# Attention in pairs of maps, with the second layer's conditioning computed inside the feed-forward stages

## The reference, cut to what matters

```
h = rms_norm(x) @ w_in          # latent c_q, c_kv, k_rope; diff q, k, v; gqa q, k, v
diff: 4 heads, each 2 maps, dim 64, value width 128
      a = softmax(q0 k0 / 8) - lam * softmax(q1 k1 / 8);  o = head_rms_norm(a @ v)
gqa:  6 query heads, 2 key/value heads, dim 64;           o = softmax(q k / 8) @ v
mla:  6 heads, q and k of dim 96, value width 64;         o = softmax(q k / sqrt(96)) @ v
x = x + concat(o) @ w_o                                   # 1280 -> 1024
x = x + (silu(xn @ w_gate) * (xn @ w_up)) @ w_down        # hidden 2816
```

## Time and profile before

| | us |
|---|---|
| median of 3 runs | 3374.56 (3374.51 to 3377.14) |
| the profiled execution's own time | 3376.07 |
| its span | 3374.3 |
| PE busy | 3199.8 (95%) |
| DVE, ACT, POOL busy | 1123.0, 994.6, 280.0 |
| chain that ended last | PE 89%, DVE 5%, ACT 4% |

### The profile page before, as it was taken

The page is one execution under the profiler, slowest core; times in us unless marked ns, Lnnn a source line. Parts: engine busy times, 40 slices in busy tenths (PEclk is TensorE's granted clock), DMA queues, the critical chain, the costliest instruction groups (busy, mean ns, idle before and its releaser), DMA issues.

```text
span 3374.3 us, 35084 instructions
## 1 busy us (share of the span) xinstructions
PE 3199.8 (95%) x14020; PEld 2222.0 (66%) x14020; DVE 1123.0 (33%) x1827; ACT 994.6 (29%) x1607; POOL 280.0 (8%) x268
## 2 busy tenths in 40 slices
PE   7999999999989999989999899979999899989997
PEld 6866564788878655648888655544666544468886
DVE  2624331433226243323332223342533300043322
ACT  3345451222233554412222133331322200022222
POOL 4481000000023610000000000000000000000000
PEclk7989999999989999999999899989999899989998
DMA  5221121332322211113323211000111122123331
GB/s 107 77 71 38 51 76 35 90 100 85 95 72 77 83 38 38 60 57 100 100 82 93 77 38 38 25 26 25 40 48 49 27 75 75 50 75 96 88 94 60
DMA packets 340274, 221.98 MB, mean 66 GB/s; under 512 B 8364, under 2 KB 334892, under 8 KB 340112
## 3 DMA queue, kind: packets, MB, share of 16 engines
q1 hardware_dynamic: 337360, 214.65, 22.0%
q0 software_dynamic: 2224, 2.99, 0.8%
q10 hardware_dynamic: 528, 2.10, 0.2%
HBM read 217.62 MB, written 2.10 MB: 65 GB/s over the span
## 4 chain that ended last, share of the span: by engine, by line
PE 89%; DVE 5%; ACT 4%; issue 1%; DMA 1%; DVEq 0%; ACTq 0%; SPq 0%
PE ps L591 83%; PE ps L602 4%; PE ps L618 2%; DVE R L1691 1%; ACT R L1204 1%; DVE xL L1687 0%; DVE x_lows L1687 0%; DMA ident<-in_c_ident 0%; PE ps L945 0%; DMA R<-in_ctx 0%; ACT R L1200 0%; ACT L1193 0%; DVE R L1780 0%; DVE R L1762 0%; DVE wL L1713 0%
## 5 line engine op out<-in xcount | busy, mean ns | idle before, releaser
L591 PE MATMUL ps<-R 128*128 128x64 f32 (+6 forms) x2272 | 519.8, 373 | 29.5 <-ACT R L1204 8.7
L591 PEld LDWEIGHTS ps<-R 128*128 128x128 f32 (+3 forms) x2272 | 306.7, 193 | 244.1 <-issue 138.1
L591 PE MATMUL ps<-xH,wH 128*128 128x512 f32 x1056 | 416.8, 395 | 22.1 <-DVE xL L1687 22.1
L1204 ACT ACTIVATE R<-ps 128x512 f32<-128x512 f32 (+9 forms) x504 | 248.4, 493 | 579.2 <-PE ps L591 514.5
L591 PE MATMUL ps<-U,ring 128*128 128x512 f32 (+5 forms) x960 | 406.3, 575 | 12.3 <-ACT R L1410 12.3
L591 PE MATMUL ps<-xL,wH 128*128 128x512 f32 x1056 | 413.7, 392 | 0.0
L591 PE MATMUL ps<-xH,wL 128*128 128x512 f32 x1056 | 413.6, 392 | 0.0
L1354 ACT ACTIVATE wH<-raws 128x2048 fp32r<-128x2048 f32 (+1 forms) x114 | 192.9, 1692 | 568.3 <-PE ps L591 567.7
L591 PEld LDWEIGHTS ps<-U,ring 128*128 128x128 f32 (+2 forms) x960 | 179.1, 191 | 207.7 <-issue 182.6
L591 PE MATMUL ps<-R,ring 128*128 128x512 f32 x704 | 311.6, 594 | 2.9 <-DVE R L1930 1.6
L1713 DVE TENSOR_TENSOR wL<-raws,wH 128x2048 fp32r<-128x2048 f32 (+1 forms) x114 | 229.3, 2011 | 233.3 <-ACT wH L1354 226.4
(11 more groups left out here) (279 smaller groups left out, 3296.1 us busy)
## 6 DMA issues: line engine op xcount, KB each, us to landing
raws<-in_w_gate_up SPq DMA_DIRECT2D x88, 512.0 KB, 5.1
ring<-in_w_in SPq DMA_DIRECT2D x36, 1024.0 KB, 6.0
ring<-in_w_ada SPq DMA_DIRECT2D x24, 1024.0 KB, 5.2
raws<-in_w_down SPq DMA_DIRECT2D x32, 704.0 KB, 4.6
raws<-in_w_ffn_in SPq DMA_DIRECT2D x44, 512.0 KB, 5.2
ring<-in_w_in SPq DMA_DIRECT2D x34, 512.0 KB, 5.6
raws<-in_w_ffn_out SPq DMA_DIRECT2D x16, 704.0 KB, 4.7
ring<-in_w_o SPq DMA_DIRECT2D x5, 1280.0 KB, 5.8
```

Source lines behind the costliest of these rows:

```text
L591: return nc.tensor.matmul(o, a, b, start=first, stop=last)
L1204: ap.do(f(dst, src, ACT.Copy), sem)
```

## The change

Attention works on pairs of maps: the two maps of a diff head, or two heads of gqa or mla, for 128 queries. That gives 16 + 12 + 12 = 40 pairs p per layer.

- **Scores.** The transposed q and k (`items`) are split like the FFN's operands, high by ACT (L1378), low by DVE, into `QK_parts`. A pair takes six fp32r matmuls of 512 columns instead of two f32 ones. In diff and gqa (dim 64) the two maps lie in the two row halves of the array and alternate. A pair writes both banks of one of two score tiles.
- **Probabilities.** In diff, DVE forms P0 + ratio P1 before the transposes, so that one map is transposed and multiplied. In gqa and mla, POOL multiplies the pair by its inverse sums (`weigh`, L624), and ACT and DVE each copy one transposed map.
- **Values.** In gqa and mla V is the stationary operand. The two heads write the two column halves of a bank, which so holds the transposed output that w_o reads. Only the four diff tiles are still transposed.
- **Order.** For each p PE has scores(p+2), probabilities(p-1), values(p-2), then the transposes of later heads (`BESIDE`) that stood between the stages. ACT has exponentials(p), the copy of p-1, and in diff the output of p-2.
- **w_in.** gqa's pieces come before the latent and diff v ones, diff head 0 is transposed after the first diff v piece, and POOL's gqa rotations stand between its last low parts.
- **Conditioning.** It leaves attention and the ring. In the FFNs of the first block, steps 5 to 36, SP loads 64 pieces of 512 KB into two halves of `spare`. POOL multiplies each by cvec and adds its eight parts to one, PE sums over the rows with one f32 matmul against a column of ones, and ACT copies one column.
- **Banks.** ACT has two PSUM banks in the first block instead of three, and three again in the second.

```diff
+        BESIDE = {-2: ["dq0", "dk0"], -1: ["dq1"], 0: ["dk1"], 3: ["dq2"], 4: ["dk2"], 7: ["dq3"], 8: ["dk3"],
+                  10: ["gk"], 11: ["gq0"], 12: ["gq1"], 13: ["gq2"],
+                  18: ["mq0"], 20: ["mk0"], 22: ["mq1"], 24: ["mk1"],
+                  26: ["mq2", "mk2"], 27: ["mq3"], 28: ["mk3"], 30: ["mq4", "mk4"], 31: ["mq5"], 32: ["mk5"]}
...
-        A_BANKS, D_BANKS, S_BANKS = psum[0:3], psum[3:5], psum[5:8]
+        psum = [ctx.enter_context(nc.psum_tensor(f"ps{i}", [P, 512], F32)) for i in range(4)]
+        SP = [ctx.enter_context(nc.psum_tensor(f"scores{i}", [P, 2, 512], F32)) for i in range(2)]
+        A_BANKS, D_BANKS = psum[0:2], psum[2:4]
...
+        ADA = [(m, 0) for m in range(16)] + [(m, 1) for m in range(16)] + [(m, 0) for m in range(16, 48)]
+        ADA_FIRST, N_ADA = 5, len(ADA) // L
...
-        W_IN = (quarter_pieces("diff_qk", c1, 2 * BH * BV) + quarter_pieces("latent", 0, c1)
-                + quarter_pieces("diff_v", c1 + 2 * BH * BV, BH * BV)
-                + quarter_pieces("gqa_q", c1 + 3 * BH * BV, GH * GD)
-                + quarter_pieces("gqa_kv", c1 + 3 * BH * BV + GH * GD, 2 * GK * GD))
...
+        W_IN = (quarter_pieces("diff_qk", c1, 2 * BH * BV)
+                + [("gqa_q", G0, GH // 2 * GD), ("gqa_q", G0 + GH // 2 * GD, GH // 2 * GD), ("gqa_kv", G0 + GH * GD, 2 * GK * GD)]
+                + quarter_pieces("latent", 0, c1)
+                + quarter_pieces("diff_v", c1 + 2 * BH * BV, BH * BV))
...
+            def weigh(l, p_):
+                a = l * N_PAIR + p_
+                r = 2 * (a % 4)
+                pg.more(sums_inverted)
+                pg.do(nc.gpsimd.tensor_tensor(PX[a % 3], PX[a % 3], bc(rinv[:, r:r + 2], S, 2), ALU.mult), weighted)
...
+            def conditioning(l):
+                pool.wait_ge(cs_ready, 1)
+                for a in range(l * N_ADA, (l + 1) * N_ADA):
+                    w = ada_half(a)
+                    pool.wait_ge(ada_in[a % 2], 16 * (a // 2 + 1))
+                    w_ = w.rearrange("p (k c) -> p k c", k=KT)
+                    pg.do(nc.gpsimd.tensor_tensor(w_, w_, bc(cvec[:, :, ADA[a][1]], P, 2), ALU.mult))
+                    for n_ in (4, 2, 1):
+                        pg.do(nc.gpsimd.tensor_tensor(w[:, 0:n_ * P], w[:, 0:n_ * P], w[:, n_ * P:2 * n_ * P], ALU.add),
+                              ada_summed if n_ == 1 else None)
...
+                    if j >= 9:
+                        rotate(pg, nc.gpsimd, j - 9, Tg, rsG, gtmp, 8, GD, gG, ropeG, gT_ready, l, 6, True)
+                rotate(pg, nc.gpsimd, 3, Tg, rsG, gtmp, 8, GD, gG, ropeG, gT_ready, l, 6, True)
...
+            def modulation(a):
+                pe.wait_ge(ada_summed, a + 1)
+                if a >= 1:
+                    pe.wait_ge(ada_read, a)
+                mm(SP[1][:, 1, 0:1], ada_half(a)[:, 0:P], ones[:, 0:1], True, True).then_inc(ada_full, 1)
...
+                def scores(p_):
+                    a, t = first + p_, p_ % TT
+                    if a >= 2:
+                        pe.wait_ge(s_exp, a - 1)
+                    pe.wait_ge(qk_ready, done + items_needed(p_))
+                    q_k, o, tok = pair_items(p_), SP[a % 2], slice(t * P, (t + 1) * P)
+                    if len(q_k) == 1:
+                        (qh, ql), (kh, kl) = [ITEM_SLOTS[item] for item in q_k[0]]
+                        for n, (q, k) in enumerate(((qh, kh), (qh, kl), (ql, kh))):
+                            for c in range(2):
+                                r = slice(c * BD, (c + 1) * BD)
+                                ins = mm(o[:, c, :], QKP[r, q, tok], QKP[r, k, :], n == 0, n == 2)
+                    else:
+                        for c in range(2):
+                            (qh, ql), (kh, kl) = [ITEM_SLOTS[item] for item in q_k[c]]
+                            for n, (q, k) in enumerate(((qh, kh), (qh, kl), (ql, kh))):
+                                ins = mm(o[:, c, :], QKP[0:AQK, q, tok], QKP[0:AQK, k, :], n == 0, n == 2)
...
+                def probabilities(p_):
+                    a = first + p_
+                    if FAMILY[p_] == "diff":
+                        pe.wait_ge(combined, l * N_DIFF + p_ + 1)
+                    else:
+                        pe.wait_ge(weighted, l * (N_PAIR - N_DIFF) + p_ - N_DIFF + 1)
+                    for c in range(1 if FAMILY[p_] == "diff" else 2):
+                        bank = A_BANKS[c]
+                        pe.wait_ge(*released[id(bank)])
+                        for s_ in range(TT):
+                            ins = nc.tensor.transpose(bank[:, s_ * P:(s_ + 1) * P], PX[a % 3][:, c, s_ * P:(s_ + 1) * P], ident[:, :])
+                        ins.then_inc(pt_full, 1)
+                        released[id(bank)] = (pt_act, a + 1) if c == 0 else (pt_dve, l * (N_PAIR - N_DIFF) + p_ - N_DIFF + 1)
...
+                def values(p_):
+                    a, i, t = first + p_, p_ // TT, p_ % TT
+                    pt = PT[a % 2]
+                    pe.wait_ge(pt_act, a + 1)
+                    if FAMILY[p_] == "diff":
+                        bank = D_BANKS[p_ % 2]
+                        pe.wait_ge(*released[id(bank)])
+                        group(None, bank[:, 0:BV], [(pt[:, 0, s_ * P:(s_ + 1) * P], V[:, s_, VB + i * BV:VB + (i + 1) * BV])
+                                                    for s_ in range(TT)]).then_inc(v_full, 1)
+                        released[id(bank)] = (v_done, v0 + p_ + 1)
+                        return
+                    n = (p_ - N_DIFF) // TT
+                    bank = D_BANKS[0]
+                    pe.wait_ge(pt_dve, l * (N_PAIR - N_DIFF) + p_ - N_DIFF + 1)
+                    if t == 0:
+                        pe.wait_ge(*released[id(bank)])
+                    for s_ in range(TT):
+                        for c in range(2):
+                            at_ = VG + c * GD if FAMILY[p_] == "gqa" else VA + (2 * (i - BH - GH // 2) + c) * AV
+                            ins = mm(bank[c * AV:(c + 1) * AV, t * P:(t + 1) * P], V[:, s_, at_:at_ + AV],
...
+                for p_ in range(N_PAIR + 2):
+                    if p_ + 2 < N_PAIR:
+                        scores(p_ + 2)
+                    if 1 <= p_ <= N_PAIR:
+                        probabilities(p_ - 1)
+                    if p_ >= 2:
+                        values(p_ - 2)
+                    beside(p_)
+                    if p_ in DIFF_OUTPUTS_AT:
+                        diff_outputs(DIFF_OUTPUTS_AT.index(p_))
...
-                pp.more(bT_ready, TT)
-                for h in range(8):
-                    transposes([T[:, t, h * P:(h + 1) * P] for t in range(TT)], P)
+                    if what == "diff_v" and a == V_AT:
+                        pp.more(bT_ready, TT)
+                        for item in BESIDE[-2]:
+                            part_transposes(l, item, (d_free, db.n))
...
+                    if ada_at(l, q) is not None:
+                        a = ada_at(l, q)
+                        if a >= 2:
+                            sp.wait_ge(ada_read, a - 1)
+                        sp.dma_start(ada_half(a).rearrange("p (k c) -> p k c", k=KT),
+                                     cols(A["w_ada_2"][0], ADA[a][0] * P, (ADA[a][0] + 1) * P)).then_inc(ada_in[a % 2], 16)
...
+                def exponentials(p_):
+                    a = first + p_
+                    act.wait_ge(s_max, a + 1)
+                    if p_ >= 3:
+                        act.wait_ge(pt_full, pt0 + banks_filled(p_ - 2))
+                    for c in range(2):
+                        n = 2 * (a % 4) + c
+                        ap.do(f(PX[a % 3][:, c, :], SP[a % 2][:, c, :], ACT.Exp, bias=nmax[:, n:n + 1], accum_out=rsum[:, n:n + 1]),
+                              s_exp if c == 1 else None)
+                def transposed(p_):
+                    act.wait_ge(pt_full, pt0 + banks_filled(p_) + 1)
+                    ap.do(f(PT[(first + p_) % 2][:, 0, :], A_BANKS[0][:, :], ACT.Copy), pt_act)
+                def diff_output(p_):
+                    h, t, r = p_ // TT, p_ % TT, 2 * ((first + p_) % 4)
+                    act.wait_ge(v_full, l * N_DIFF + p_ + 1)
+                    ap.do(f(O[:, t, h * BV:(h + 1) * BV], D_BANKS[p_ % 2][:, 0:BV], ACT.Copy, scale=rinv[:, r:r + 1]), v_done)
+                for item in BESIDE[-1]:
+                    high(l, item)
+                for p_ in range(N_PAIR + 2):
+                    if p_ < N_PAIR:
+                        exponentials(p_)
+                    if 1 <= p_ <= N_PAIR:
+                        transposed(p_ - 1)
+                    if 2 <= p_ < N_DIFF + 2:
+                        diff_output(p_ - 2)
...
+                def rowmax(p_):
+                    a = first + p_
+                    dve.wait_ge(s_full, a + 1)
+                    n = 2 * (a % 4)
+                    vp.do(v.tensor_reduce(nmax[:, n:n + 2], SP[a % 2][:, :, :], AX.X, ALU.max, negate=True), s_max)
+                def inverses(p_):
```

(59 more changed lines are left out.)

476 lines of the change are left out of this document (243 added, 233 removed).

## The result

| | before | after |
|---|---|---|
| median of 5 runs, us | 3377.14 (3374.51 to 3382.41) | 3404.99 (3396.44 to 3412.51) |
| ratio, 95% interval | | 1.0083 (1.0071 to 1.0095) |
| span of the profiled execution | 3374.3 | 3403.5 |

What follows compares the result with a forecast made beforehand. PE, busy 95% of the span, bounded the kernel; afterwards a PE-ACT chain would set attention's beat. 3376 - 34 - 12 - 9 + 16 + 15 + 2 = 3354, or 3352 against the median; range 3295 to 3425.

Steps and rivals of the forecast that it cites:

- The chain: Attention: each pair runs through PE and ACT in turn; 4.9 us a diff pair, 4.15 gqa, 4.62 mla at full clock.
- -34 for attention: Both attention stages: 255 us a layer, 510 in all, against 544.4 before.
- a third of attention at half clock: Attention: the assumed share of time with PE's clock at half, giving 255 us a layer.
- own two ends, 230 and 300: Attention, us per layer: 230 with PE at full clock, about 300 with the clock at half.
- rival 3: Attention: clock at half for three quarters of it, as PE idles every cycle; 283 us a layer, about 3408; chance 0.22.
- Conditioning, +15: First-block FFNs: 64 f32 matmuls on one column at 0.24 us each; +15 us, bounds +7 and +25.
- rival 5: FFN: weights come late behind SP's wait at `ada_read`, and POOL holds DVE's port; +40 us, 3392; chance 0.05.
- Rotations, +16: Ahead of attention: DVE's diff rotations slowed by POOL's gqa rotations, and PE waits; +16 us, bounds 0 and +45.
- -12: Ahead of the up-projections: most diff tile transposes leave and PE waits less; -12 us, bounds 0 and -14.
- Output tiles, -9: Beside w_o: none of ten output tiles is transposed there any more; -9 us, bounds -5 and -12.
- Banks, +2: Two ACT banks in place of three; +2 us, bounds 0 to +10.
- Rival 4: Attention scores: row halves of fp32r matmuls don't overlap; +37 us, so 3389; chance 0.08.

Runs made afterwards that it cites:

- the filler's kernel: The changed kernel with three more f32 matmuls of 256 columns behind the work of each of 37 pairs a layer; 3361.2 us, ratio 0.9963.
- rotations last: The changed kernel with POOL's gqa rotations back behind the last low part, as before the change; 3392.3 us, ratio 1.0052.
- the kernel before once more: The kernel before the change, unchanged and profiled again for its second block; that block repeated its 1498.7 us to 0.1 us.
- scores last: The changed kernel with PE's order in an attention pair made transposes, values, then the scores of p+2; 3244.5 us, ratio 0.9613.

## Why the prediction was wrong

The likeliest case was 3352 and faster. It came out 3405 and slower, inside the stated range, on the side to which 0.37 was given.

- **What bounds attention.** Right. The chain was named with its order, and its cycles were sized to within a us. For a diff pair at half clock 6.8 us was worked out and 7.4 with an item. At a granted clock of 0.50 throughout, the trace has 6.54 between the scores of two pairs (332.60 to 339.14); with an item it has 7.62 (312.73 to 320.35), at 0.65 in the mean. At full clock a gqa pair takes 3.9, for 4.15 expected, an mla pair 4.5, for 4.62, and an mla pair with an output tile's transposes 6.5, for 6.8. Small slips in the terms (scores are 0.66 and 0.36, so 1.02 and not 1.04; PE's end to ACT is 0.26 and not 0.30) change nothing.
- **The term that failed: -34 for attention.** It rests on "a third of attention at half clock". The stages' clocks of 0.77 and 0.73 mean that 46% and 54% of the time was at half. The row leant on, with 5.85 of 8.00 us busy at 1.00, was too short to stand for a stage. Attention came out 268 us a layer instead of 255, which is 26 of the missing 51 us. The prediction's own two ends, 230 and 300, give 265 with half of the time at half clock, and 237 with a tenth, as in the filler's kernel, where 268 and about 233 were measured. So the chain was sized rightly and the share of half clock was not. It was rival 3 in kind, at half its size (its limit of 272 is 60% of the time at half clock, not a bare majority). The filler shows that PE's gaps are the cause.
- **What I should have drawn from it.** The point was not the clock but the order. I had PE's own work at 2.4 to 3.1 us a pair and the chain at 4.2 to 4.9, and took the chain as given. Scores stand first in PE's list and alone wait for ACT. Transposes and values, ready a pair earlier, stand behind them.
- **Conditioning, +15.** The matmuls cost 15.4. The edit cost 24 (8.4 in the up halves and 15.8 in the down halves), and what was missed is the SP queue. "The wait ends within the step, so it costs nothing while the raws' lead is over it" is the step that failed: rival 5, given 0.05 and priced at 40. It holds in the up halves, where a step is 10.6 us, and not in the down halves, where it is 7.3. I had one sentence for both. Of rival 5's two reasons, POOL's hold on the port played no part.
- **Rotations, +16.** Mechanism right. Undoing it gives 12.7. What remained of the part ahead of attention was then +1.1 (183.2 and 175.1 against 179.4 and 177.8), where **-12** had been taken for transposes that leave. They did leave: the up-projections and what was between fell by 6.8 us. The rest went into the w_in stages, which even with rotations last are 7.9 longer than before. Of that 5.8 is idle time of PE and 2.1 its work, among it the transposes of the first diff head, which now stand there. The w_in stages before:

```profile
42.80:191.90 149.10, 146.17 (x1021) 133.86 (x1022) 72.88 (x100) 56.15 (x97) 78.81 (x56) 0.96 0.38 80
970.40:1119.90 149.50, 146.53 (x1021) 134.24 (x1022) 70.44 (x88) 56.16 (x97) 47.70 (x11) 0.95 0.23 69
```

- **Output tiles, -9:** -7.2.
- **Banks, +2:** no stage shows it apart, and no run has three banks there.
- **The second block, 0:** +7.1. It goes with the clock. PE is busy for 1406.2 us with the same instructions that took 1397.4 (the row of the kernel before once more, above), and its idle time did not grow:

```profile
1897.50:3403.50 1506.00, 1406.23 (x5018) 883.21 (x5017) 456.27 (x763) 343.20 (x491) 8.38 (x9) 0.94 0.21 56
```

  Why the clock is lower there stays open. One thing that the change alters for this block is its PSUM banks, ACT's third being now half of a score tile; that was not tried apart. The clearest piece is PE at 0.54 of the clock for 10 us, on work that ran at full clock before, with no gap in either. First before, then after:

```profile
2575.60:2585.60 10.00, 10.00 (x57) 8.70 (x56) 2.30 (x4) 3.66 (x6) 0.00 (x0) 1.00 0.01 2
```

```profile
2597.50:2607.50 10.00, 10.00 (x35) 8.00 (x34) 1.65 (x3) 2.56 (x4) 0.00 (x0) 0.54 0.01 2
```

- **Rival 4 is excluded.** Six row-half scores take 0.89 us at full clock (275.42 to 276.31), where one after the other they would be 1.32. The row halves overlap in fp32r too, and 1.04 had been worked out.

In sum, against 3354 for the profiled execution: attention +26.3, conditioning +9.2, the part ahead of attention +9.2, the second block +7.1, output tiles +1.8. Less the 2 forecast for the banks and the 0.4 by which the first stage starts earlier, that is 51 us, and 3405.3 less 3354 is 51.3.

## What to carry to other kernels

When each pair of engines' work is worked out, and the chain comes out longer than either engine's own, look at the order in the lists before the size of the work: an instruction that waits for the other engine belongs behind those that are ready. That order was worth 160 us here, the clock that it gave back included, more than the 149 us by which the change shortened PE's busy time.

A gap on PE is to be priced twice, with its own length and with the clock of what follows: here the clock's part was 26 to 31 us a stage or more. And a load put into an existing queue brings its wait with it. It is harmless where the step is long and not where it is short, so look at the shortest step.

## What the hardware showed that I had not expected

- More work made it faster: 222 MATMUL instructions more in a stage, 26 to 31 us less, at a clock of 0.95 instead of 0.75. That rule of the Trainium skill (TensorE: Matmul & The Clock Gate, Part 4) by which transposes do not count as TensorE being busy in the same way was not tested: the fillers were plain matmuls, and no run here had transposes in their place. The prediction's use of it, that gqa's pairs would be at half clock, did not come true. In the changed kernel gqa (second row), with eight transposes a pair, had 0.85, and diff (first row), with four, had 0.69:

```profile
231.30:350.50 119.20, 73.54 (x357) 56.98 (x356) 54.37 (x83) 53.07 (x120) 40.42 (x42) 0.69 0.04 10
350.50:397.40 46.90, 31.44 (x240) 22.72 (x240) 25.70 (x37) 22.43 (x47) 14.76 (x8) 0.85 0.00 1
```

- The clock of a stage may not follow the busy share alone. With 76 and 77% busy the stages of the kernel with scores last ran at 0.90, and the filler's with 78% at 0.95. The shares lie close, so this is a hint and not shown.
- PE's clock can be at half in one kernel and full in another on the same work with no gap before it, at the same place in repeated runs. The 10 us that begin 700 us into the second block had 1.00 in both profiles of the kernel before, and 0.50 to 0.62 in the changed kernel and in all eight variants that keep three banks there.
